# A layer kernel whose first projection takes x times the norm's feature weights, with the norm's factor per token put in after it

## The reference, cut to what matters

```
h = rms_norm(x, norm_mix)                 # x * rsqrt(mean(x*x) + eps) * gain
proj = h @ w_in
rq, rk, rv, rg, dq, dk, dv = split(proj)
rq = rotary(rq, pos)
rk = rotary(rk, pos) * (64 ** -0.5)
o_ret = rms_norm(retention_chunkwise(rq, rk, rv)) * silu(rg)
dq = rms_norm(dq, diff_q_gain)            # per head of 64
dk = rms_norm(dk, diff_k_gain)
o_diff = diff_attention_causal(dq, dk, dv, lam)
...
```

## Time and profile before

| | us |
|---|---|
| median of 3 runs | 2281.15 |
| lowest, highest run | 2280.82, 2284.95 |
| profiled execution, its own time | 2280.16 |
| its span | 2278.3 |
| PE busy in the span | 2218.7 (97%) |
| POOL busy | 1296.7 (57%) |
| DVE busy | 1312.9 (58%) |
| ACT busy | 959.0 (42%) |

### The profile page before, as it was taken

The page is one execution under the profiler, slowest core; times in us unless marked ns, Lnnn a source line. Parts: engine busy times, 40 slices in busy tenths (PEclk is TensorE's granted clock), DMA queues, the critical chain, the costliest instruction groups (busy, mean ns, idle before and its releaser), DMA issues.

```text
span 2278.3 us, 34847 instructions
## 1 busy us (share of the span) xinstructions
PE 2218.7 (97%) x12540; PEld 1920.9 (84%) x12540; DVE 1312.9 (58%) x2104; ACT 959.0 (42%) x1490; POOL 1296.7 (57%) x1440
## 2 busy tenths in 40 slices
PE   7999999999999999999999999999989999999997
PEld 6778787678888879999999989877777887999997
DVE  4525632598878778454554655234247546877666
ACT  3354644444233454332332343255546535444443
POOL 3434465199988766554644634333346164887775
PEclk9999999999999999999999999999999999999999
DMA  4322142355555542222212222222230021333232
GB/s 157 104 81 84 56 133 90 111 175 198 198 188 199 186 148 74 66 65 74 75 58 73 75 74 72 75 88 81 67 105 29 20 102 60 98 101 104 95 110 75
DMA packets 67952, 229.27 MB, mean 101 GB/s; under 512 B 7264, under 2 KB 12640, under 8 KB 67680
## 3 DMA queue, kind: packets, MB, share of 16 engines
q1 hardware_dynamic: 50944, 176.67, 23.1%
q10 hardware_dynamic: 16864, 50.60, 6.7%
HBM read 224.36 MB, written 2.10 MB: 99 GB/s over the span
## 4 chain that ended last, share of the span: by engine, by line
PE 81%; DVE 8%; issue 5%; ACT 3%; POOL 3%; DMA 0%; ACTq 0%; POOLq 0%; DVEq 0%; SPq 0%
PE ps L2343 19%; PE ps L2853 11%; PE ps L2347 10%; PE ps L2912 7%; PE ps L2908 7%; PE ps L2909 7%; PE ps L3062 4%; PE ps L2399 3%; POOL WLO L455 2%; PE ps L2354 1%; PE ps L3004 1%; PE ps L3182 1%; PE ps L3033 1%; PE ps L3047 1%; PE ps L3200 1%
## 5 line engine op out<-in xcount | busy, mean ns | idle before, releaser
L455 POOL TENSOR_TENSOR WLO<-RAW,WHI 128x256 fp32r<-128x256 f32 x996 | 865.2, 904 | 708.6 <-ACT WHI L553 708.0
L553 ACT ACTIVATE WHI<-RAW 128x1024 fp32r<-128x1024 f32 x249 | 260.6, 1056 | 275.2 <-DMA RAW<-in_stream_dram 266.6
L474 POOL TENSOR_TENSOR WLO<-RAW,WHI 128x256 fp32r<-128x256 f32 x240 | 235.5, 1002 | 196.4 <-DVE SRAW L1941 77.7
L2343 PE MATMUL ps<-HLO,WHI 128*128 128x512 f32 (+2 forms) x848 | 306.6, 378 | 0.0
L2343 PE MATMUL ps<-HHI,WHI 128*128 128x512 f32 (+2 forms) x848 | 300.5, 371 | 0.0
L2347 PE MATMUL ps<-HHI,WLO 128*128 128x512 f32 (+2 forms) x848 | 192.5, 371 | 0.3 <-POOL WLO L455 0.3
L2343 PEld LDWEIGHTS ps<-HLO,WHI 128*128 128x128 f32 (+1 forms) x848 | 154.7, 188 | 32.4 <-issue 4.3
L2343 PEld LDWEIGHTS ps<-HHI,WHI 128*128 128x128 f32 (+1 forms) x848 | 154.9, 188 | 30.4 <-issue 2.6
L2347 PEld LDWEIGHTS ps<-HHI,WLO 128*128 128x128 f32 (+1 forms) x848 | 149.3, 188 | 28.3 <-POOL WLO L455 0.5
L2853 PE MATMUL ps<-GLO,WHI 128*128 128x384 f32 (+1 forms) x480 | 143.7, 353 | 1.3 <-POOL WLO L455 1.1
L2853 PE MATMUL ps<-GHI,WHI 128*128 128x384 f32 (+1 forms) x480 | 143.5, 353 | 0.0
(11 more groups left out here) (508 smaller groups left out, 5333.9 us busy)
## 6 DMA issues: line engine op xcount, KB each, us to landing
RAW<-in_stream_dram SPq DMA_DIRECT2D x329, 512.0 KB, 3.3
ADA<-in_ada_dram ACTq DMA_DIRECT2D x72, 512.0 KB, 4.0
BM<-in_bias_dram ACTq DMA_DIRECT2D x8, 448.0 KB, 3.9
DECAY<-in_decay_dram ACTq DMA_DIRECT2D x4, 512.0 KB, 3.7
C<-in_ctx_dram ACTq DMA_DIRECT2D x2, 1024.0 KB, 5.5
out_dram<-X SPq DMA_DIRECT2D x16, 128.0 KB, 1.8
X<-in_x_dram SPq DMA_DIRECT2D x2, 512.0 KB, 5.9
X<-in_x_dram ACTq DMA_DIRECT2D x2, 512.0 KB, 6.9
```

Source lines behind the costliest of these rows:

```text
L455: op = nc.gpsimd.tensor_tensor(WLO[:, slot(u), k:k + 2], RAW[:, slot(u), k:k + 2], WHI[:, slot(u), k:k + 2].bitcast(F32), ALU.subtract)
L474: op = nc.gpsimd.tensor_tensor(WLO[:, j, k:k + 2], RAW[:, j, k:k + 2], WHI[:, j, k:k + 2].bitcast(F32), ALU.subtract)
L553: nc.scalar.activation(WHI[:, j], RAW[:, j], ACT.Copy).then_inc(unit_hi, 1)
L2343: nc.tensor.matmul(out, high[k], x[:, k, tok], start=(k == 0 and n == 0), stop=False)
```

## The change

- HHI is made from x times gain straight away (`mix_hi`, ACT, from the SBUF tile X), without r. HLO is X times gain minus HHI (`mix_low`, DVE, both tensor inputs in SBUF).
- The squares and their sum come interleaved with this; r is summed by PE in the middle of `ret_value(0)`, after its token blocks 0 and 1 (`mix_totals`: one matmul of 512 columns, and four of 2 columns that give r with tokens on partitions).
- r enters later: DVE multiplies COS and SIN by r (tile RSX), ACT scales the value copies per token (`token_rs`), DVE multiplies each gate product by r before Silu reads it, DVE multiplies each differential query and key product by r in its PSUM bank before it is squared (`diff_scale`), and DVE scales the copies of the differential values.
- SP issues x tiles 0 and 1, `vec`, unit 0, x tiles 4 and 5, constants, units 2 and 3, tables. ACT issues x tiles 2 and 3, unit 1, x tiles 6 and 7.
- PE runs 24 matmuls on a tile of zeros ahead of everything. Units 0 and 1 are projected with all their WHI terms first, then the WLO terms.

The diff, cut to its core:

```diff
@@ SP
-            for i in range(2):
+            for i in (0, 2):
                 sp.dma_start(X[:, 2 * i:2 * i + 2], ...).then_inc(x_landed[i], 16)
-            for u in range(WSLOTS):
...
+                if i == 0:
+                    sp.dma_start(vec[:], t["vec"]).then_inc(vec_landed, 16)
+                    sp.dma_start(RAW[:, 0], t["stream"][0]).then_inc(unit_landed[0], 16)
+            sp.dma_start(const[:], ...).then_inc(const_landed, 16)
+            for u in range(2, WSLOTS):
                 sp.dma_start(RAW[:, u], t["stream"][u]).then_inc(unit_landed[u], 16)
@@ ACT
+            def mix_hi(k):
+                act.wait_ge(x_landed[k // 2], 16)
+                nc.scalar.activation(HHI[:, k, 0:S], X[:, k], ACT.Identity, scale=vec[:, ...]).then_inc(s("norm_hi"), 1)
...
+            nc.scalar.activation(ps[:, 3], ps[:, 3], ACT.Ln, scale=1.0 / D, bias=eps).then_inc(s("norm_ln"), 1)
+            nc.scalar.activation(small[:, 8:16], ps[:, 4, 0:8], ACT.Ln, scale=1.0 / D, bias=eps).then_inc(s("token_rs"), 1)
             act.wait_ge(*norm_at("n1", "ln", 1))
+            nc.scalar.activation(RSX[:], ps[:, 3], ACT.Exp, scale=-0.5).then_inc(s("norm_rs"), 1)
+            act.wait_ge(s("token_rs"), 1)
+            nc.scalar.activation(small[:, 8:16], small[:, 8:16], ACT.Exp, scale=-0.5).then_inc(s("token_rs"), 1)
...
-                for b in range(2):
-                    nc.scalar.activation(VN[:, 2 * b:2 * b + 2, v], ps[...], ACT.Copy).then_inc(s("ret_v"), 1)
+                for b in range(QT):
+                    op = nc.scalar.activation(VN[:, b, v], ps[:, bank, c0:c0 + 2 * P], ACT.Identity, scale=token_rs(b))
...
-                nc.scalar.activation(SG[:], ps[:, 7 if i + 1 < RET_PAIRS else 6], ACT.Silu).then_inc(s("ret_gate"), 1)
+                act.wait_ge(s("ret_scaled"), i + 1)
+                nc.scalar.activation(SG[:], SG[:], ACT.Silu).then_inc(s("ret_gate"), 1)
@@ DVE
+            V.memset(KR[:, 0:P], 0.0).then_inc(eps_set, 1)
-                V.tensor_tensor(HLO[:, k, 0:S], ps[:, 3 + k % 2], HHI[:, k, 0:S].bitcast(F32), ALU.subtract)
+                V.scalar_tensor_tensor(HLO[:, k, 0:S], X[:, k], col("norm_mix", k), HHI[:, k, 0:S].bitcast(F32), ALU.mult, ALU.subtract)
...
+            for table in (COS, SIN):
+                V.tensor_tensor(table[:], table[:], RSX[:], ALU.mult).then_inc(s("lam_prod"), 1)
+            dve.wait_ge(s("lam_prod"), 4)
             ret_rope(0)
+            def diff_scale(j):
+                wait_unit(UNIT["diff_qk"] + j)
+                V.tensor_tensor(ps[:, j % 4], ps[:, j % 4], RSX[:], ALU.mult).then_inc(s("ret_scaled"), 1)
...
+                V.tensor_tensor(SG[:], ps[:, 7 if i + 1 < RET_PAIRS else 6], RSX[:], ALU.mult).then_inc(s("ret_scaled"), 1)
...
-                    V.tensor_copy(DV[:, 2 * b:2 * b + 2, ...], ps[:, 2 * a + b]...)
+                    op = V.tensor_scalar(DV[:, b, ...], ps[...], token_rs(b), None, ALU.mult)
@@ PE
-            sum_of("n1", TN[:, 0], wait=4)
-            spin(0, 9)
-            pair(RET_Q[0], 0, ...)
+            pe.wait_ge(eps_set, 2)
+            for _ in range(24):
+                nc.tensor.matmul(ps[:, 0, 0:P], KR[:, 0:P], KR[:, 0:P], start=True, stop=True)
+            for k in range(KD):
+                pe.wait_ge(*norm_at("n1", "hi", k + 1))
+                for b in range(2):
...
+                    nc.tensor.matmul(ps[:, 5 + b], WHI[:, b, k], HHI[:, k, x_tok], start=(k == 0), stop=False)
+                pe.wait_ge(*norm_at("n1", "lo", k + 1))
+                for b in range(2):
+                    nc.tensor.matmul(ps[:, 5 + b], WHI[:, b, k], HLO[:, k, x_tok], start=False, stop=False)
+            for b in range(2):
+                wait_weights(RET_Q[0] + b)
+                for k in range(KD):
+                    mm = nc.tensor.matmul(ps[:, 5 + b], WLO[:, b, k], HHI[:, k, x_tok], start=False, stop=(k == KD - 1))
...
-            ret_value(0)
-            ret_value(1)
+            ret_value(0, (0, 1), False)
+            mix_totals()
+            ret_value(0, (2, 3), True)
+            ret_value(1, range(QT), True)
```

More of the change, by code:

```diff
@@ L411, in build, with token_rs @@
         subln_coef = small[:, 4:8]
+        def token_rs(b):
+            return small[:, 8 + 2 * b:9 + 2 * b]
         block = ctx.enter_context(nc.Block())
@@ L617, in _, with mix_square @@
+            def mix_hi(k):
                 act.wait_ge(x_landed[k // 2], 16)
+                nc.scalar.activation(HHI[:, k, 0:S], X[:, k], ACT.Identity, scale=vec[:, VEC["norm_mix"] + k:VEC["norm_mix"] + k + 1]
+                                     ).then_inc(s("norm_hi"), 1)
+            def mix_square(k):
                 square("n1", SQ, k, k, [(X[:, k], 0, S)])
+            mix_hi(0)
             convert(0)
+            mix_hi(1)
             convert(1)
+            mix_hi(2)
+            mix_hi(3)
@@ new lines, in _ @@
+            mix_square(0)
+            mix_hi(4)
+            mix_square(1)
+            mix_hi(5)
+            mix_hi(6)
+            mix_hi(7)
+            mix_square(2)
+            convert(2)
+            mix_square(3)
+            convert(3)
+            for k in range(4, KD):
+                mix_square(k)
+            act.wait_ge(const_landed, 16)
+            for a, c in enumerate((IDENT, CAUSAL)):
+                nc.scalar.activation(constr[:, a], const[:, c], ACT.Copy).then_inc(s("constr"), 1)
@@ L2436, in _, with ret_value, mix_totals @@
             x_tok = slice(0, S)
-            def ret_value(v):
+            def ret_value(v, blocks, last):
                 unit_tokens([2 * v + 2, 2 * v + 3], 0,
-                            [(ps[:, ((0, 1), (2, 7))[v][a // 2], 256 * (a % 2):256 * (a % 2) + 256], slice(a * P, (a + 1) * P)) for a in range(QT)],
-                            hi=HHI, lo=HLO)
+                            [(ps[:, ((0, 1), (2, 7))[v][a // 2], 256 * (a % 2):256 * (a % 2) + 256], slice(a * P, (a + 1) * P)) for a in blocks],
+                            hi=HHI, lo=HLO, last=last)
+            def mix_totals():
+                acc = TN[:, 0]
+                pe.wait_ge(const_landed, 16)
+                pe.wait_ge(*norm_at("n1", "acc", KD + 1))
+                nc.tensor.matmul(ps[:, 3], const[:, ONES], acc, start=True, stop=True)
+                for b in range(QT):
+                    mm = nc.tensor.matmul(ps[:, 4, 2 * b:2 * b + 2], acc[:, b * P:(b + 1) * P], const[:, ONES, 0:2], start=True, stop=True)
+                mm.then_inc(s("norm_ms"), 1)
             def ret_scores(i):
```

128 lines of the change are left out of this document (62 added, 66 removed).

## The result

The changed kernel took **2291.55 us** (median of 8 runs, 2286.6 to 2294.63) against 2283.41 for the kernel before on the same chips (8 runs): ratio 1.004, 95% interval 1.0031 to 1.0049, and 8.1 us between the medians. It is slower by 0.4%, as the forecast said in sign; but 2291.55 lies outside the range that ended at 2289, and the added time is about twice the +4.1 us of the sum. Not all of the distance is the change's: the forecast was added to 2281.15, the median of 3 runs, and with 8 runs the median of before is 2283.41. Of the 6.35 us between 2285.2 and 2291.55, 2.26 lie in this base. The profiled execution took 2292.68, its span 2290.9.

The account below looks back on a forecast made before the run. It took the start of ret_value(1), behind unit 4's conversion and POOL's WLO, as the moment that decides: +2.2 for its later start and +1.9 for PE's clock make +4.1, on 2281.15 giving 2285.2 us; range 2277 to 2289.

Parts of the forecast that it names:

- Start: First weights: unit 0 lands at 9.3 and is converted in 1.06; POOL starts at 10.4 instead of 14.29, 3.9 us gained.
- POOL beside DVE: POOL's units 0 to 3: 14 DVE instructions cost POOL 0.45 each, 6.3 us in all, so POOL ends at 27.8.
- Rival 4: POOL's first stretch: each DVE instruction holds POOL up for its whole time, 4.3 us more, 2289.5; chance 0.05.
- rival 1: POOL's first units: POOL and DVE hardly meet, units 0 to 3 done at 23.2; −4.2 us, 2277.0; chance 0.10.
- Token blocks 0 and 1 are 48 matmuls … so 5.9: First part of ret_value(0): 48 matmuls at 0.122 take 5.9 us, ending at 33.8.
- rival 2: Ahead of the norm's sum: PE falls to half rate earlier too, up to 3 us more; +7.1, 2288.3; chance 0.18.
- ACT's list behind the sum: Between the norm's sum at 35.7 and unit 4's conversion at 37.9: ACT's work there takes 2.2 us.
- From there to PE: From unit 4's conversion to ret_value(1): 6.9 us plus 1.8 for ret_rope(0) beside POOL; start at 46.6, 2.2 later.
- The gap and its clock: Ahead of ret_value(1): PE idles 5.0 us instead of 1.79, and the clock behind it costs 1.9 us.
- rival 3: Ahead of ret_value(1): the 5.0 us gap leaves the clock alone; +2.2, 2283.4; chance 0.14.
- The eight diff_scale … PE needs only after the next unit, 5.4 later: Differential query and key units: 0.69 each between a unit and its square, counted among edits of no cost.
- What follows shifts along, unless a new wait enters there: After ret_value(1) starts: earlier changes are worth only what they do to that moment; new waits after 60 us would disprove.

Follow-up runs that it names:

- e5: Changed kernel with squares and HLO taken through PSUM, so no DVE instruction beside POOL's first four units has two SBUF inputs: 2287.46 us, ratio 1.0024 to before.
- e1: Changed kernel with ACT converting units 4 and 5 ahead of its wait for the norm's sum: 2283.67 us, ratio 1.001 to before.
- e4: Changed kernel with the fourth unit's total of the first q/k turn taken after the next turn's first unit: 2291.86 us.
- e9: Changed kernel with the edits of e1 and e4 together: 2281.98 us, ratio 1.0003 to before.
- a_cb_first: Changed kernel with the load of CB issued ahead of that of C: 2286.84 us, ratio 1.0021 to before.
- a_again2: Changed kernel run again unchanged, for a third profile: 2288.98 us.
- e3: Changed kernel with unread matmuls filling PE's gaps, 8 ahead of ret_value(0) and 20 ahead of ret_value(1): 2286.11 us, ratio 1.0018 to before.
- a_again: Changed kernel run again unchanged, for a second profile: 2293.45 us.
- b_again: Kernel before the change run again unchanged, for a second profile: 2283.65 us.
- e7: Changed kernel with the edits of e1, e5 and e4 together: 2278.93 us, ratio 0.9989 to before.
- e6: Changed kernel with the edits of e1 and e4, and of e5 only the squares through PSUM: 2278.03 us, ratio 0.9987 to before.

## Why the prediction was wrong

Step by step, the forecast's number and then the trace's, of the profiled execution of after:

- Start: conversion 9.3, 9.25; POOL 10.4, 10.38. Right.
- POOL beside DVE: end 27.8, 27.84, by 14 meetings of 0.45. Right, and shown by e5: 6.26 us go without them. Rival 4, the hold for a whole instruction, would have added 14 × 0.69 = 9.7 us instead of 6.3, and falls. The Trainium skill's page "SBUF — State Buffer" says, in its section "SBUF: two separate sides", that of a DVE instruction with two SBUF inputs and a GpSimd one that reads SBUF, whichever starts first gets the shared ports for its whole instruction while the other fully blocks; the trace, with 0.45 a meeting, does not agree with that for these shapes.
- `ret_value(0)`: 27.9, 27.99. Right; rival 1 (23 to 25) falls.
- **"Token blocks 0 and 1 are 48 matmuls … so 5.9"**: this step failed. They took 7.3. The wait of 2.0 ahead of them, which the prediction itself had worked out, was followed by half rate. That is rival 2's place and its sign (it decides "if blocks 0 and 1 take over 7 us"), at 1.4 us instead of "up to 3". I gave it 0.18; the profiles of after show it in two of three, and so do those of e1, e4, e9 and a_cb_first, which leave this place alone. In the third, a_again2, the blocks take 5.8 behind the same wait, and the shift at 100 is +4.2 against a forecast of +4.1:

```profile
28.10 0.36 PE L2444 MATMUL ps<-WLO,HHI 128*128 128x256 f32 x1 [2.01 <-POOL WLO L461]
...
33.92 1.02 PE L2493 MATMUL ps<-TN,const 128*128 128x512 f32 x2
```

- ACT's list behind the sum: 2.2, 2.0 (37.2 to 39.21). From there to PE: 8.7, 8.64, with POOL at 7.36 for 5.6 + 1.8. Right.
- The gap and its clock: 5.0 and 1.9, 4.89 and 2.02. Right; rival 3 falls. e3 shows both half rates apart from the rest.
- **"The eight diff_scale … PE needs only after the next unit, 5.4 later"**: wrong for the fourth unit of the first turn, whose total has no unit behind it. +0.75, shown by e4. I had looked at the rule for three units and not at the turn's last.
- **"What follows shifts along, unless a new wait enters there"**: this failed too. The wait of 2.2 to 2.9 us near 490 comes in every execution of the changed kernel and its versions with the loads of C and CB in this order, and in one of four of before. After also runs at half rate more often late in the span, which may be chance. Together about 2 us by the medians; how the change brings the wait about is not shown.

Sum: 4.1 + 1.4 + 0.75 = 6.25, the measured shift at 190 of 6.3; the rest of the 8 us is the last point. On the base of 3 runs, 2281.15, these 6.25 us alone would have ended at 2287.4, inside the range; the base, 2.26 low, and the last point together carried the time past its end. (The forecast's own range has a slip: its ±0.4 is in the upper end, 2286.7, and not in the lower, which would be 2283.6. Nothing rests on it.) The direction came out of a mechanism that was right; its size was low because one rival was treated as an alternative to the forecast when it adds to it, because of an overlooked wait, and because the range took the 2200 us behind, and the base of 3 runs, as fixed.

## What to carry to other kernels

When a stage is started earlier, look at what now stands behind its last wait on each engine's list: here two conversions in ACT's list, moved ahead of one wait, were worth 7 us, more than the four us that the early start had promised. A wait that the sum itself brings out (2.0 us of PE ahead of dense matmuls) needs a clock term of its own, added with its chance, not put aside as a rival. For every "hidden behind the next unit", look at the unit that has no next one.

## What the runs showed of the hardware that was not expected

- The same wait is followed by half rate in one execution and not in another: 2.0 us at 26 to 28 in after and a_again (matmuls 0.21 apart, granted clock 0.83 over 26 to 36), not in a_again2 (28.10, blocks in 5.8, clock 1.00 over the same stretch); 3.45 near 1680 in two of four profiles of before, and a wait of 0.99 near 254 in one of four (b_again). What decides it cannot be read from the wait's length in these rows.
- A kernel's times go with the clock: in the 8 runs of after the span's mean granted clock was 0.997 for 2286.6 us and 0.992 for 2294.63.
- Taking a contention away altogether was worse than taking half of it: HLO through PSUM freed POOL by 2.9 us (e7 against e6) and moved the start of `ret_value(0)` from 24.84 to 26.45, since DVE then made HLO late.
